# Feed-forward up projections by seven block products per tile in place of eight, and the down projection in four spans, in a one-core decoder layer

## The reference

```python
def swiglu(x, w1, w3, w2):
    return (jax.nn.silu(x @ w1) * (x @ w3)) @ w2

def ffn_half_step(x, w1, w3, w2, g, b):
    return layer_norm(ALPHA * x + 0.5 * swiglu(x, w1, w3, w2), g, b)
...
hp = ffn_half_step(xp, ffn1_w1, ffn1_w3, ffn1_w2, ln1_g, ln1_b)
mp = mixer(hp)          # one input projection, pooling branch, windowed attention, gates, w_out
hp = layer_norm(ALPHA * hp + mp, ln2_g, ln2_b)
xp = ffn_half_step(hp, ffn2_w1, ffn2_w3, ffn2_w2, ln3_g, ln3_b)
```

## Time and profile before

| | |
|---|---|
| runs | 1166.99, 1168.55, 1381.94 us; median 1168.55 |
| profiled execution | span 1165.2 us; its own time is not listed apart |
| PE / DVE / ACT / POOL busy | 98% / 48% / 32% / 13% of the span |
| matmul and transpose records | 8774 |
| chain that ended last | PE 91%, DVE 6%, ACT 2% |

### The profile page before, as it was taken

One profiled execution on the slowest core, in us unless ns is written; L12 is line 12 of the kernel. 1 busy time (PEld: TensorE's weight loads), 2 busy tenths in 40 slices (PEclk: granted clock), 3 DMA queues, 4 the chain that ended last, 5 costly groups with the idle time before them and its releaser, 6 DMA issues.

```text
span 1165.2 us, 21801 instructions
## 1 busy us (share of the span) xinstructions
PE 1136.7 (98%) x8774; PEld 1110.7 (95%) x8774; DVE 556.8 (48%) x957; ACT 376.4 (32%) x676; POOL 149.6 (13%) x171
## 2 busy tenths in 40 slices
PE   6999999999999999999999999799999999999996
PEld 6999999999999989998899999699999999999994
DVE  3343433243443486877455555943443324444347
ACT  5222222122133334374442243422222222223334
POOL 2000000000002468400000015500000000000240
PEclk9999999999999989999999999999999999999998
DMA  9233441233333243221132332133243213234102
GB/s 250 73 91 90 124 134 56 73 91 91 95 107 88 70 120 74 76 64 37 46 91 73 96 105 78 50 91 89 78 119 94 73 56 109 79 90 132 43 1 77
DMA packets 191416, 101.16 MB, mean 87 GB/s; under 512 B 15129, under 2 KB 189453, under 8 KB 191320
## 3 DMA queue, kind: packets, MB, share of 16 engines
q1 hardware_dynamic: 189136, 95.77, 28.8%
q0 software_dynamic: 2208, 4.38, 1.2%
HBM read 97.63 MB, written 3.68 MB: 87 GB/s over the span
## 4 chain that ended last, share of the span: by engine, by line
PE 91%; DVE 6%; ACT 2%; issue 1%; DMA 0%; SPq 0%; DVEq 0%; ACTq 0%
PE psum L1157 29%; PE psum L1159 29%; PE psum L1158 28%; DVE y L868 1%; DVE act_lo L875 1%; PE psum L1341 1%; DVE y L849 1%; DVE ring_lo L788 1%; DVE stat L854 1%; PE psum L1357 1%; ACT ring_hi L528 0%; DMA xin<-in_x_prompt 0%; PE psum L1373 0%; DVE y L813 0%; PE psum L1269 0%
## 5 line engine op out<-in xcount | busy, mean ns | idle before, releaser
L1157 PE MATMUL psum<-act_hi,ring_hi 128*128 128x272 f32 x1824 | 532.0, 292 | 8.8 <-DVE act_lo L875 4.9
L1159 PE MATMUL psum<-act_hi,ring_lo 128*128 128x272 f32 x1824 | 530.3, 291 | 0.0
L1158 PE MATMUL psum<-act_lo,ring_hi 128*128 128x272 f32 x1824 | 527.0, 289 | 0.0
L1157 PEld LDWEIGHTS psum<-act_hi,ring_hi 128*128 128x128 f32 x1824 | 345.6, 189 | 17.7 <-DVE act_lo L875 9.3
L788 DVE TENSOR_TENSOR ring_lo<-raw,ring_hi 128x1024 fp32r<-128x1024 f32 (+1 forms) x170 | 202.0, 1189 | 305.7 <-ACT ring_hi L528 258.8
L1158 PEld LDWEIGHTS psum<-act_lo,ring_hi 128*128 128x128 f32 x1824 | 346.3, 190 | 0.0
L1159 PEld LDWEIGHTS psum<-act_hi,ring_lo 128*128 128x128 f32 x1824 | 345.4, 189 | 0.0
L528 ACT ACTIVATE ring_hi<-raw 128x1024 fp32r<-128x1024 f32 (+1 forms) x170 | 172.4, 1016 | 234.7 <-PE psum L1159 232.6
L568 ACT ACTIVATE tmp_a<-psum 128x272 f32<-128x272 f32 x184 | 73.2, 398 | 424.4 <-PE psum L1159 363.6
L1157 PE MATMUL psum<-hid_hi,ring_hi 128*128 128x272 f32 x512 | 148.6, 290 | 0.0
L1158 PE MATMUL psum<-hid_lo,ring_hi 128*128 128x272 f32 x512 | 147.0, 287 | 0.0
(11 more groups left out here) (185 smaller groups left out, 1184.6 us busy)
## 6 DMA issues: line engine op xcount, KB each, us to landing
raw<-in_ffn_w SPq DMA_DIRECT2D x176, 256.0 KB, 3.2
raw<-in_ffn_w SPq DMA_DIRECT2D x32, 512.0 KB, 4.0
raw<-in_w_in SPq DMA_DIRECT2D x52, 256.0 KB, 3.3
ext_raw<-in_ffn_w SPq DMA_DIRECT2D x32, 192.0 KB, 4.1
raw<-in_w_out SPq DMA_DIRECT2D x16, 256.0 KB, 3.2
raw<-in_w_pool_out SPq DMA_DIRECT2D x16, 128.0 KB, 2.3
raw<-in_w_attn_out SPq DMA_DIRECT2D x16, 128.0 KB, 2.7
xin<-in_x_prompt SPq DMA_DIRECT2D x3, 512.0 KB, 5.7
```

The source lines that it names most:

```text
L1157: pe.matmul(o, weights(s, k, True), x_hi[:, k, tok(c)], start=k == 0, stop=False)
L1158: pe.matmul(o, weights(s, k, True), x_lo[:, k, tok(c)], start=False, stop=False)
L1159: ins = pe.matmul(o, weights(s, k, False), x_hi[:, k, tok(c)], start=False, stop=k == kn - 1)
```

## The change

**Seven products.** For a hidden tile f the two weights side by side are a 2 x 2 block matrix (channels 0-511 or 512-1023, by `w1` or `w3`), the activations another one (token half by the same channel halves). Before, that was eight block products of 4 chunks each (12 matmuls). In tiles 2 to 21 it is now seven (`PRODUCTS`: M1, M2, M3, M5, M6, M4, M7 in PE's order). For it: 
- DVE forms once per feed-forward four sums of activation blocks `xs` (128 x 1088 each), ACT and DVE split them into `xs_hi` and `xs_lo` (`token_sums`, L1143 to L1151).
- POOL forms four weight sums `wsum` of 512 elements per partition for each tile (`wsums`, L604 to L611), from `raw`.
- ACT and DVE split three sets of 1024 and one of 512 elements per tile (G0 to G3, `split_set`) where they split two of 1024. There is one set of seven weight tiles, refilled piece by piece as the products finish.
- M6 and M7 accumulate onto M1's bank, with a read between them. ACT copies M2, M5 and M4 out of PSUM (`copy`), and DVE adds (`R1` after M2, `R2` and `R5` after M6, `R3` and `R4` after M7): R1 and R3 are the arguments of the SiLU for the two token halves, R5 and R4 the factors. M6 may not start before R1, nor M7 before R2.
- the rounding of the hidden tile moves from DVE to ACT (`hidden_hi`).

Tiles 0 and 1 (`PLAIN`) stay as eight products, and stand first: token half 0 of both, then token half 1 of both, in eight banks.

**Four spans.** The hidden width goes in spans of 6, 6, 5, 5 tiles, each followed by a down projection of 8 x 2 parts with 18 or 15 matmuls a part, in three banks. Only the first span's parts pass through ACT; in the others DVE adds out of PSUM with the factor 0.5. The hidden tiles of one span take the place of those of the last. The norm's work stands beside the last span.

**No loops.** All programs of the feed-forwards are written out.

```diff
-KF = FF // P // 2
+NF = FF // P
+DOWN = KD
+PLAIN = 2
+SPANS = ((0, 6), (6, 12), (12, 17), (17, 22))
...
+            def wsums(l, f):
...
+                if f > PLAIN:
+                    pool.wait_ge(lo_done, split_at(l, "G", f - 1, 2) + 1)
...
+                for n in (n0, n1):
+                    pool.wait_ge(raw_in[n % RAWS], 32 * (n // RAWS + 1))
+                pool.tensor_tensor(wsum[:, 0], w12, w11, ALU.subtract).then_inc(wsum_done, 1)
+                pool.wait_ge(wsum_done, done + 1)
+                pool.tensor_tensor(wsum[:, 1], w22, wsum[:, 0], ALU.subtract).then_inc(wsum_done, 1)
+                if f > PLAIN:
+                    pool.wait_ge(lo_done, split_at(l, "G", f - 1, 3) + 1)
+                pool.wait_ge(wsum_done, done + 2)
+                pool.tensor_tensor(wsum[:, 2], w21, wsum[:, 1], ALU.subtract).then_inc(wsum_done, 1)
+                pool.tensor_tensor(wsum[:, 3], w22, w12, ALU.subtract).then_inc(wsum_done, 1)
...
+            def seven(l, f):
...
+                product(bank, *tiles[0], top_hi, top_lo, onto=False).then_inc(part_done, 1)
...
+                product(both, *tiles[1], low_hi, low_lo).then_inc(part_done, 1)
...
+                product(ups, *tiles[2], xs_hi[:, 2], xs_lo[:, 2]).then_inc(part_done, 1)
...
+                product(gates, *tiles[3], xs_hi[:, 0], xs_lo[:, 0]).then_inc(part_done, 1)
+
+                pe.wait_ge(sum_done, sums_at(l, f, "R1"))
+                product(bank, *tiles[4], xs_hi[:, 1], xs_lo[:, 1], onto=True).then_inc(part_done, 1)
+
+                pe.wait_ge(lo_done, split_at(l, "G", f, 3) + 1)
+                pe.wait_ge(copied, copied_at(l, f, "M2"))
+                product(both, *tiles[5], end_hi, end_lo).then_inc(part_done, 1)
+
+                pe.wait_ge(sum_done, sums_at(l, f, "R2"))
...
+                product(bank, *tiles[6], xs_hi[:, 3], xs_lo[:, 3], onto=True).then_inc(part_done, 1)
```

More of the change, by code:

```diff
@@ new lines, in load_counts, with split_counts @@
+def load_counts():
+    at = {}
+    for j, (f0, f1) in enumerate(SPANS):
+        for f in range(f0, f1):
+            for w in range(2):
+                at["S", f, w] = len(at)
+        for o in range(DOWN):
+            at["D", j, o] = len(at)
+    return at
+def split_counts():
+    at = {}
+    for j, (f0, f1) in enumerate(SPANS):
+        for f in range(f0, f1):
+            for w in range(2 if f < PLAIN else 4):
+                at["W" if f < PLAIN else "G", f, w] = len(at)
+        for o in range(DOWN):
+            at["D", j, o] = len(at)
+    return at
@@ L278, in sq_slot, with wo_splits @@
             return 4 * c + (o if o < 4 else 1 + (o - 4) % 3)
[L280 to L289, removed]
+        def wo_splits(s, fourth=False):
+            if s < DOWN:
+                return [WO_BASE + s + 2] if s + 2 < DOWN else []
+            return []
         SQ_OPS = KD - 2
@@ L449, in _ @@
                 pool.dma_start(out[name][0, :, 0:n - DS], a[src][0, :, DS:n]).then_inc(side_stored, 16)
+            for f in range(SPANS[0][1], NF):
+                wsums(0, f)
             def add_bias(l):
@@ L513, in _ @@
             add_bias(1)
+            for f in range(PLAIN, NF):
+                wsums(2, f)
             all_norm_sums(2)
@@ L930, in ffn @@
                                 norm_reciprocal(l, 0)
-                            if half == 1 and s == DOWN + 1:
+                            if s == DOWN + 1:
                                 norm_scale(l, 0)
-                            for u in splits(b, s):
-                                split(u, unit_kind(u))
+                        if s + 3 < DOWN:
+                            split_down(l, j, s + 3)
+                        if j < LASTJ and 6 <= s < 9:
+                            split_set(l, f1, s - 6)
@@ L936, in _ @@
+                        if j == LASTJ and l == 0:
+                            for u in {6: (0,), 7: (1,), 9: (2,)}.get(s, ()):
+                                split(u, KD)
             split_act(0)
-            split(1, KD)
-            split(2, KD)
+            split_plain(0, 0, 1)
+            split_plain(0, 1, 0)
             split_act(1)
-            ffn(0, 0, 0)
+            ffn(0)
             def rotate(u, c, dst):
@@ new lines, in ffn @@
+            def ffn(l):
+                for c in range(2):
+                    for f in range(PLAIN):
+                        if l == 2 and c == 0:
+                            pe.wait_ge(evac[f], MIX_UNITS)
+                        plain(l, f, c)
+                        if l == 0 and c == f == 0:
+                            for i in range(3, len(TOK_TILES)):
+                                turn_in(i)
+                            pe.wait_ge(turn_read, len(TOK_TILES))
+                    if l == 0 and c == 0:
```

790 lines of the change are left out of this document (541 added, 249 removed).

## The result

The changed kernel takes 1147.18 us (median of 4 runs, 1145.4 to 1148.06) beside 1167.71 for the kernel before (median of 3 runs, 1166.99 to 1168.55); the ratio on record is 0.9828, 95% interval 0.9816 to 0.9839. One execution of the kernel before (1381.94 us) and one of e10 (1497.08 us) fell into a slow state of the chip and are left out of every comparison. The change makes the kernel faster by 1.7%, which is within 2%. Forecast were 1137.0, range 1119 to 1175, and a gain of over 2% had the larger chance (0.60; within 2% had 0.33). Of the 63 us that the matmuls and loop turns free, 31.5 were to be given back; 42 are.

The account below looks back on a forecast made before the run. PE was taken as the bound, one matmul per 0.125 us. From 1168.55, -63 for work removed, +8 tiles, +11.5 and +3 starts, +9 ends make -31.5, so 1137.0 us; range 1119 to 1175.

Parts of the forecast that it names:

- The class: Whole kernel: chance 0.60 of faster by over 2%, 0.33 of within 2%, 0.07 of slower by over 2%.
- What goes: PE: 480 matmuls of 0.125 us and 16 loop turns of 0.2 us leave, together -63 us.
- Tiles, 8 us: Strassen tiles: DVE's cycle taken as 10.8 us against PE's 10.5 over 40 tiles, less slack, costing 8 us.
- the 0.6 of the forecast: Tiles: DVE may lag 0.6 us before M7 waits, credited once in each of 8 spans.
- rival 1: Tiles: DVE softly becomes the bound, cycle 11.3 us, 1156 us in all, deciding from 11.0; chance 0.27.
- The lock: DVE and POOL: operations with two SBUF inputs exclude each other; DVE sums reading PSUM run free beside POOL.
- Start of feed-forward 2, 11.5 us: First M1 of feed-forward 2 waits 9.8 us for G0, then loses 1.8 us at half clock.
- Start of feed-forward 1, 3 us with bounds 0 and 6: First M1 of feed-forward 1: G0 ready at 44 to 45, PE at 42.1, costing 3 us.
- the same chain starts when DVE ends the token splits at 26.8: Feed-forward 1: the chain to G0 begins at 26.8 and takes 28.5 + 10.5 + 2.8 + 2.3, to 44 to 45.
- Ends, 9 us: Last down spans: POOL trails 1 us at each statistics, 2 together; later scaling costs +4 and +3.
- Rival 3: Whole kernel: nothing is late, tiles at 10.5, starts 8 + 0, ends 3, giving 1116.5 us; chance 0.15.
- rival 2: Tiles: the lock hides nowhere, DVE's cycle 12.2 us, slower kernel at 1203.6 us; chance 0.08.

Follow-up runs that it names:

- e10: Changed kernel without most POOL weight and norm sums and without token sums, second token half's transposes back between the first two products: 1115.04 us, ratio 0.9554.
- e1: Changed kernel with nearly all of POOL's weight sums left out from the second Strassen tile on: 1138.19 us, ratio 0.9760.
- e11: Changed kernel with R2 and R5 of a tile placed between the next tile's G0 and G1 on DVE: 1146.93 us, ratio 0.9825.
- e8: Changed kernel without the token sums and their splits, products reading plain activation blocks instead: 1130.13 us, ratio 0.9690.
- e6: Changed kernel with starts reordered: G0 before low parts, R2 and R5 earlier, token sums before first product, transposes back between first two products: 1143.2 us, ratio 0.9794.
- e9: Changed kernel with nearly all of POOL's norm sums behind the two feed-forwards left out: 1144.28 us, ratio 0.9802.
- e4: Changed kernel with spans of 5, 5, 6, 6 tiles in place of 6, 6, 5, 5: 1143.58 us, ratio 0.9798.
- e3: Changed kernel with the first Strassen tile's G0 split ahead of the low parts of the token sums: 1147.3 us, ratio 0.9833.
- e5: Changed kernel with POOL's first weight sums of feed-forward 2 waiting for DVE's four token sums: 1146.42 us, ratio 0.9819.
- e12: Changed kernel with the starts' order of e6, the spans of e4 and the swap of e11 together: 1135.45 us, ratio 0.9732.

## Why the forecast was 10 us off

- **The class: the less likely one.** A gain of over 2% had a chance of 0.60; the measured 1.7% is within 2% (0.33). The terms below say why: tiles and ends came nearly as summed, the starts did not, and some 5 us lie outside every term.
- **What goes: right.** 8294 matmuls; e10's pace is 0.125 us and it comes within 11 us of the bound of 1105.
- **Tiles, 8 us: right in size, in part by luck, by a cycle of 11.0 and not 10.8.** e1 gives 7.9 and shows that it is POOL's sums. Two errors cancel: steady tiles lose 0.5 and not 0.3, and each span wins back more than the 0.6 of the forecast, since its last tile (no sums beside it) takes 9.9. By the forecast's own sum a cycle of 11.0 would have cost 15. 11.0 is also the point from which rival 1 was to decide, and M7 waited for R2, its sign: DVE is indeed the bound of a tile (e11), softly, and the spans are too short for it to cost more. Busy some 70% was forecast for DVE in a steady tile; it is 93% (10.26 of 11.01), POOL 50% (5.56). POOL's sum of 512 elements takes 1.27 unblocked, where 1.09 was taken from two neighbours. The page GPSIMD Engine Reference of the Trainium skill (3.1 Elementwise) gives 2.6 cycles per element, by estimate 1.11 us ahead of any dispatch; the trace's 1.27 lies above it, as that wants.
- **The lock: right.** Both orders, DVE behind POOL (158.33) and POOL behind DVE (751.55, 2.22 us), are in the rows, and PSUM sums take 0.43 beside POOL's sum. The Trainium skill (SBUF — State Buffer, Who interferes with whom) holds here too.
- **Start of feed-forward 2, 11.5 us: right in mechanism, short in size.** PE waits 12.0 for G0, not 9.8, and loses 2.0, not 1.8, at half clock: 14.0.
- **Start of feed-forward 1, 3 us with bounds 0 and 6: wrong.** This is the step that failed: "the same chain starts when DVE ends the token splits at 26.8". The diff moves the transposes behind both first products, which makes these splits end at 31.7, and the token sums stand in DVE's queue behind the first product, which waits for ACT's copy of the vectors and a table load (first SiLU at 34.9). Sums at 36.65, G0 at 49.7, M1 at 50.97: 8.9 us behind PE's forecast 42.1, and 2.4 of slow clock. By the runs both starts together cost about 19 to 21 us (e8's 16.1, the 2.9 of R2 waits that it opens, up to 2 of the transposes), where 14.5 was forecast; the trace's own lateness, 25.3, counts some time that other waits would have taken. e6 takes only 4.0 of it back by order, so the place in the queue was a part of the fault and the work itself the larger one.
- **Ends, 9 us: right.** POOL trails by 3 (e9, known to 3; in the trace PE's waits for it are 2.0, forecast 2), and 6.4 are DVE's chain of 7.1 us behind parts of 1.9, forecast 7: +4.2 in feed-forward 1 (+4) and +2.1 in 2 (+3). e10 leaves it, and no run takes it out; e4 shows the price per part: 2.25 us parts give back 3.5.
- **The sum.** Tiles 8, starts 20, ends 9, 2 at the first products of feed-forward 1 and 3 unnamed: 42 given back of 63. The forecast started from 1168.55, which is 0.8 above the 1167.71 of the result. Rival 3 had assumed that nothing is late, rival 2 a cycle of 12.2; neither happened.

## What to carry over

When work is moved from the bounding engine to its helpers, first write down how long each helper's queue is at the start and at the end of a phase: in the middle this kernel lost 8 us in 40 tiles, at four phase edges 30. An operation in order on a queue inherits the wait of the one ahead of it; the token sums needed nothing from the SiLU they stood behind. And where two engines exclude each other, another order mostly moves the wait (e3 and e5 gained 0 to 1 us, e11 nothing in its time and some 2 in its trace); less work of that kind, or cover with work that doesn't share (idle time, longer parts), shortens it. Before a microsecond or two is explained, look whether a stretch that nobody touched has changed as much (e12).
